# Sample attention reordered: scores of four requests together, values two groups behind, page loads split over two queues

## What is computed

```
# 8 query heads x 64, 2 KV heads, 4 query rows per request: 32 query rows per request
compressed: s = q . kc^T over 255 compressed blocks; p = softmax(s)
            p_grp = sum of p over the 4 heads of a KV head; p_slc = p_grp @ overlap
selected:   idx = top 16 of 65 blocks of 64 tokens (first, last two are forced)
            softmax(q . k^T) . v over the tokens of those blocks, out of 4096 cached and the new ones
window:     softmax(q . k^T) . v over the last 512 cached tokens and the new ones
o = g0 * o_compressed + g1 * o_selected + g2 * o_window
```

## Time and profile before

| | us |
|---|---|
| median of three runs | 3051.97 (3051.2 to 3059.78) |
| the profiled execution | 3054.68 |
| its span, first to last instruction | 3052.6 |
| prompt attention ends (POOL's last instruction) | 1871.5 |
| constants stage, first DMA issue | 1872.6 |
| sample attention, first DMA issue | 1878.0 |
| output projection, first DMA issue | 2109.2 |

### The profile page before, as it was taken

The page is one execution under the profiler, slowest core; times in us unless marked ns, Lnnn a source line. Parts: engine busy times, 40 slices in busy tenths (PEclk is TensorE's granted clock), DMA queues, the critical chain, the costliest instruction groups (busy, mean ns, idle before and its releaser), DMA issues. The chain is left out here.

```text
span 3052.6 us, 46122 instructions
## 1 busy us (share of the span) xinstructions
PE 2769.7 (91%) x17724; PEld 2539.2 (83%) x17724; DVE 1461.4 (48%) x2801; ACT 912.7 (30%) x1600; POOL 343.8 (11%) x362
## 2 busy tenths in 40 slices
PE   4999989999999999899688885876999999999997
PEld 4898978999999999799566663333989999999996
DVE  4444437444444544641377674122264444444445
ACT  4656544111111110323366563333041111111102
POOL 3444430000000000000022223110000000000000
PEclk9999999999999999999789897888999999999999
DMA  4222215111111210213110114544131111111101
GB/s 169 75 102 101 76 65 154 42 41 46 50 41 41 59 37 0 90 58 95 35 47 28 43 42 157 177 145 140 35 97 42 41 41 52 45 41 41 55 0 57
DMA packets 169425, 206.40 MB, mean 68 GB/s; under 512 B 11310, under 2 KB 152495, under 8 KB 166410
## 3 DMA queue, kind: packets, MB, share of 16 engines
q1 hardware_dynamic: 161074, 150.68, 16.2%
q0 software_dynamic: 8224, 54.06, 4.9%
HBM read 190.87 MB, written 18.01 MB: 68 GB/s over the span
## 5 line engine op out<-in xcount | busy, mean ns | idle before, releaser
L406 ACT ACTIVATE f_act_gate<-f_act_gate 128x352 f32<-128x352 f32 x132 | 65.8, 498 | 1186.2 <-DVE f_act_gate L463 1186.2
L500 DVE SCALAR_TENSOR_TENSOR trunk<-f_down,trunk 128x352 f32<-128x352 f32 x528 | 276.0, 524 | 207.6 <-PE f_down L104 207.6
L102 PE MATMUL f_up<-f_h_hi,f_gu_hi 128*128 128x352 f32 x1056 | 344.5, 326 | 0.0
L102 PE MATMUL f_gate<-f_h_hi,f_gu_hi 128*128 128x352 f32 x1056 | 344.3, 326 | 0.0
L104 PE MATMUL f_up<-f_h_hi,f_gu_lo 128*128 128x352 f32 x1056 | 342.7, 325 | 0.0
L104 PE MATMUL f_gate<-f_h_hi,f_gu_lo 128*128 128x352 f32 x1056 | 342.5, 324 | 0.0
L102 PE MATMUL f_down<-f_a_hi,f_wd_hi 128*128 128x352 f32 x1056 | 340.6, 323 | 0.0
L103 PE MATMUL f_gate<-f_h_lo,f_gu_hi 128*128 128x352 f32 x1056 | 340.5, 322 | 0.0
L103 PE MATMUL f_up<-f_h_lo,f_gu_hi 128*128 128x352 f32 x1056 | 340.1, 322 | 0.0
L103 PE MATMUL f_down<-f_a_lo,f_wd_hi 128*128 128x352 f32 x1056 | 338.4, 320 | 0.0
L104 PE MATMUL f_down<-f_a_hi,f_wd_lo 128*128 128x352 f32 x1056 | 338.0, 320 | 0.0
(11 more groups left out here) (359 smaller groups left out, 5457.8 us busy)
## 6 DMA issues: line engine op xcount, KB each, us to landing
as_pages<-in_cache_kv_slc_dram SPq DMA_DIRECT2D x192, 128.0 KB, 2.3
f_gu_raw<-in_w_ffn_gate_dram SPq DMA_DIRECT2D x44, 512.0 KB, 4.2
f_gu_raw<-in_w_ffn_up_dram SPq DMA_DIRECT2D x44, 512.0 KB, 5.5
f_wd_raw<-in_w_ffn_down_dram SPq DMA_DIRECT2D x22, 1024.0 KB, 5.0
at_spread<-saved_rows SPq DMA_DIRECT2D x16, 768.0 KB
as_pages<-in_cache_kv_slc_dram POOLq DMA_DIRECT2D x64, 128.0 KB, 3.4
x_saved<-trunk SPq DMA_DIRECT2D x2, 2112.0 KB, 13.4
trunk<-x_saved SPq DMA_DIRECT2D x1, 4224.0 KB
```

What stands on the lines that cost most here:

```text
L102: pe.matmul(out, w_hi, x_hi, start=first, stop=False)
L406: act.activation(act_gate[:, b, :], act_gate[:, b, :], ACT.Silu).then_inc(silu_done, 1)
L500: dve.scalar_tensor_tensor(xT[:, m, chunk(c)], down_bank[n % 4][:, 0:CH], 0.5, xT[:, m, chunk(c)], ALU.mult, ALU.add).then_inc(down_free, 1)
```

## The change

`stage_attend_sample` is written anew.

- **Order.** The loops over halves and rounds are gone. 18 steps (`STEPS`) run in one straight line: the window of half 0, page groups 0 to 4 of half 0, the window of half 1, page groups 5 to 7 of half 0, then the 8 page groups of half 1. The compressed scores, head sum, choice of blocks and norms of half 1 are put between page groups of half 0, and half 0 is finished (`finish`, `flip`, `place`) during page groups of half 1.
- **Scores.** There are four `kT`, one per request. The step's transposes go in two pairs, and the four score matmuls are issued one behind the other at the end of the step (`key_scores`). ScalarE copies the transposed keys of requests 0 and 1, VectorE those of 2 and 3 (`take_keys`).
- **Values.** The products of step n-2 (`values_of`) stand between the two pairs of transposes of step n. The transposes of the probabilities of step n-1 stand ahead of the scores of step n.
- **Side branch.** The eight small value units become two units of up to 512 columns.
- **Page loads.** SP loads requests 0 and 1, POOL requests 2 and 3: 32 batches each. Page-table addresses are constants, the page numbers are read ahead of the wait for the slot, and the slot is free when the products have been made. The states of half 1 are loaded behind the third page group.
- **Ahead.** `kc`, the gates, `head_sum` and `new_mask` are loaded by SP at the start of prompt attention, and the eight new rows are copied there too. `stage_constants` before sample attention is gone. `win_mask` is loaded at the start of sample attention.
- **Waits.** The idle instructions that TensorE issued to signal the end of a group are gone. Each matmul of a group signals for itself.

The core of the diff:

```diff
             @block.sync
             def _(sp):
+                for target, source in loads_ahead:
+                    sp.dma_start(target, source).then_inc(ahead, 16)
+                for target, source in rows_out:
+                    sp.dma_start(target, source).then_inc(copied, 16)
                 for n in range(TILES):
...
+    SHARE = RQ // 2
+
+    STEPS = ([("w", 0, None)] + [("p", 0, g) for g in range(5)] + [("w", 1, None)]
+             + [("p", 0, g) for g in range(5, KG)] + [("p", 1, g) for g in range(KG)])
...
+    CMP_STEP = [0, 4]
+    SUM_STEP = [0, 5]
+    FLIP_STEP = [LAST_STEP[0] + 4, None]
...
-        kT = [mem.sb(scope, f"as_kT{i}", [P, BANK]) for i in range(2)]
+        kT = [mem.sb(scope, f"as_kT{b}", [P, BANK]) for b in range(RQ)]
...
+        def load_pages(engine, kind, first_request, landed, p):
+            h, g = divmod(p, KG)
+            for b in range(first_request, first_request + SHARE):
+                first = (RQ * h + b) * NP + GP * g
+                _, numbers = nc.values_load_multi_w_load_instructions(
+                    pages[0:1, first:first + GP], [kind], min_val=0, max_val=cache_slc.shape[0] - 1)
+                if p >= RING and b == first_request:
+                    engine.wait_ge(pv_done, values_counted(p - RING))
+                for j, page in enumerate(numbers):
+                    engine.dma_start(page_ring[p % RING][:, b, j, :],
...
-                sp.dma_start(kc[:], kc_dram).then_inc(kc_landed, 16)
+                sp.dma_start(win_mask[:], win_mask_dram).then_inc(mask_landed, 16)
                 sp.dma_start(vc[:], vc_dram).then_inc(vc_landed, 16)
...
-                load_pages(sp, mybir.EngineType.SP, range(RQ - 1), pages_landed)
+                for p in range(PAGES):
+                    load_pages(sp, mybir.EngineType.SP, 0, pages_landed, p)
...
-                load_pages(pool, mybir.EngineType.Pool, [RQ - 1], last_pages_landed)
+                load_state(pool, 0)
+                for p in range(PAGES):
+                    load_pages(pool, mybir.EngineType.Pool, SHARE, more_landed, p)
+                    if p == RING - 2:
+                        load_state(pool, 1)
...
+                exp_cmp(0)
+                for n in range(N):
+                    if n == WIN_STEP[0] + 1:
+                        exp_of(n - 1)
+                    for b in range(SHARE):
+                        take_keys(n, b)
+                    if n > WIN_STEP[0] + 1:
+                        exp_of(n - 1)
+                    if n:
+                        probs_of(n - 1)
+                    if n == CMP_STEP[1]:
+                        exp_cmp(1)
+                exp_of(N - 1)
+                probs_of(N - 1)
...
+                def take_keys(n, b):
+                    dve.wait_ge(kt_turned, RQ * n + b + 1)
+                    dve.wait_ge(s_done, RQ * n)
+                    dve.tensor_copy(kT[b][:], kt_bank[b % 2][:]).then_inc(kt_by_dve, 1)
...
+                for n in range(N):
+                    if n:
+                        max_of(n - 1)
+                    if n == WIN_STEP[0] + 1:
+                        choose_blocks(0)
+                        win_norm(0)
+                    for b in range(SHARE, RQ):
+                        take_keys(n, b)
+                        if b == SHARE and n >= 2:
+                            take_out(n - 2)
...
+                def key_scores(n):
+                    h = STEPS[n][1]
+                    pe.wait_ge(kt_by_act, SHARE * (n + 1))
+                    pe.wait_ge(kt_by_dve, SHARE * (n + 1))
+                    if n >= 2:
+                        pe.wait_ge(s_taken, n - 1)
                     for b in range(RQ):
...
+                        pe.matmul(s_bank[n % 2][rows_of(b), :], queries(RQ * h + b), kT[b][:],
+                                  start=True, stop=True).then_inc(s_done, 1)
...
+                for n in range(N):
+                    if n == CMP_STEP[1]:
+                        cmp_scores(1)
+                    if n == FLIP_STEP[0]:
+                        flip(0)
+                    for b in range(SHARE):
+                        turn_keys(n, b)
+                    if n >= 2:
+                        values_of(n - 2)
+                    for b in range(SHARE, RQ):
+                        turn_keys(n, b)
+                    if n == SUM_STEP[1]:
+                        sum_heads(1)
+                    if n:
+                        probs_of(n - 1)
+                    key_scores(n)
+                values_of(N - 2)
+                probs_of(N - 1)
+                values_of(N - 1)
+                flip(1)
...
+                loads_ahead = [(kc[:], kc_saved), (K["head_sum"][:], c_head_sum), (K["new_mask"][:], c_new_mask)]
+                loads_ahead += [(gate[rows * (b % 4):rows * (b % 4 + 1), b // 4, :],
...
-            stage_constants(nc, mem, [(K["head_sum"][:], c_head_sum), (K["new_mask"][:], c_new_mask),
-                                      (K["win_mask"][:], c_win_mask)] + new_rows)
```

More of the change, by code:

```diff
@@ L2100, in stage_attend_sample @@
[L2100 to L2116, removed]
+        kt_turned, kt_by_act, kt_by_dve = mem.sem("as_kt_turned"), mem.sem("as_kt_by_act"), mem.sem("as_kt_by_dve")
@@ L2118, in stage_attend_sample, with load_state @@
+        def load_state(engine, h):
+            for b in range(RQ):
+                engine.dma_start(state[h][:, b], state_win[RQ * h + b].rearrange("(w p) n -> p w n", p=P)
+                                 ).then_inc(state_landed[h], 16)
         with nc.Block() as block:
@@ L2371, in value_product @@
-                def value_product(hb, n, i, rows, values, bank, first, last):
-                    pe.wait_ge(pt_taken, UNITS * hb + n + RING_TOKENS + 1)
-                    for b in range(RQ):
-                        mm = pe.matmul(bank[ROWS * b:ROWS * (b + 1), 0:P], pT[i][0:rows, ROWS * b:ROWS * (b + 1)],
-                                       values(b), start=first, stop=last)
-                    mm.then_inc(pv_done, 1)
-                def turn_group(hb, g, k):
-                    n = SIDE + 1 + g
-                    pe.wait_ge(exped, SOFT * hb + g + 4)
-                    pe.wait_ge(pt_taken, UNITS * hb + n + 1)
-                    for j in range(GP):
-                        tr = pe.transpose(pt_bank[(SIDE + 1 + k) % 2][:, j * P:(j + 1) * P],
-                                          p_page[k % 2][:, j * P:(j + 1) * P], K["ident"][:])
-                    tr.then_inc(pt_turned, 1)
@@ new lines, in products @@
+                def products(u, bank, terms, first, last, counted=True):
+                    for i, (rows, at, values) in enumerate(terms):
+                        for b in range(RQ):
+                            mm = pe.matmul(bank[rows_of(b), 0:P], pT[u % 2][0:rows, at + ROWS * b:at + ROWS * (b + 1)],
+                                           values(b), start=first and i == 0, stop=last and i == len(terms) - 1)
+                            if counted and i == len(terms) - 1:
+                                mm.then_inc(pv_done, 1)
@@ L2672, in trunk_step @@
         mem.end_stage()
-        with ExitStack() as mixer:
+        ahead, rows_copied = mem.lasting_sem("loaded_ahead"), mem.lasting_sem("rows_copied")
+        with ExitStack() as mixer, ExitStack() as late:
             z_sample = mem.sb(mixer, "z_sample", [P, OFF_POOL])
```

522 lines of the change are left out of this document (275 added, 247 removed).

## The result

The changed kernel takes 0.9708 of the time of the kernel before (95% interval 0.9694 to 0.9723): a median of 2966.3 us against 3054.3, 4 runs each. Run a second time beside other kernels it gave 0.9705 (0.9688 to 0.9722). The profiled execution took 2973.97 us with a span of 2972.1. It was the slowest of its four: prompt attention took 374.7 us in it, and 368.4 in the second profile of the same kernel, against 369.4 before.

What follows compares the result with a forecast made beforehand. Before, a chain of one request after another bound sample attention; after, POOL's page-load issue would. 3054.68 - 5.46 (constants stage) - (231.2 - 144.7) (sample attention) = 2962.7, taken as 2960 us against the runs' median; range 2942 to 2992.

Steps and rivals of the forecast that it cites:

- The constants stage: Ahead of sample attention: removing it saves 5.46 us, its DMA issue moved into SP's idle time in prompt attention at 0 cost.
- The scores side by side: Score matmuls of a step: four requests' pairs run together in 0.9 us plus run-out, with 3.6 as the other bound.
- The step of 5.5 us: Sample attention's new order: one step of computation at full clock, from scores to next scores, takes 5.5 us.
- The computation's floor of 127 us: Sample attention without load limits: 13 + 6 + 93.5 + 5 + 9.6 = 127 us, against 231.2 before.
- POOL sets the pace: Sample attention's page loads: POOL's 32 batches at 3.7 us give 7.4 us per page group, stage 144.7 us; chance 0.62.
- The sign named for POOL's pace: In the profile after: TensorE's third transposes of a step wait for POOL's pages, steps 7.4 us apart.
- The 3 us added for steps that run late: Sample attention: 3 us added to the stage for steps late behind the window steps or at the lower clock, giving 144.7.
- The ring holds: Page slots: 14.8 us from a slot's release to its next use, for 7.4 of issue and 3.4 of landing.
- Rival 1: Sample attention: computation sets the pace through a lower clock or scores in turn, step 8.2 us, time 2991; chance 0.18.
- Rival 2: Page loads: POOL's issue gets dearer under VectorE's copies, 0.67 us per batch, 21 us in all, time 2982; chance 0.07.
- Rival 3: Page loads: POOL's issue is cheaper in straight-line code and not the bound, computation's 127 us stands, time 2942; chance 0.08.
- Rival 4: Slower through the ring: pages landing in above 17.6 us make steps above 12.5 us; 3082 at 20 us landing; chance 0.03.

Runs made afterwards that it cites:

- e8: The changed kernel with a constants stage ahead of sample attention again (head_sum, new_mask, eight new rows): 0.9739 of the kernel before.
- e4: The changed kernel with each of a step's four score matmuls waiting until the one before has ended: 0.9854 of the kernel before.
- e1: The changed kernel with only the first four page groups loaded, all computation kept, output not the reference's: 0.9666 of the kernel before.
- e12: The changed kernel with five slots instead of four in the ring of pages, nothing else: 0.9694 of the kernel before.
- e10: The changed kernel with values behind all four transposes, accumulation behind both key copies, and no bounds checks of page numbers: 0.9712 of the kernel before.
- e11: The changed kernel with values behind all four transposes, accumulation behind both key copies, no bounds checks and a ring of five: 0.9667 of the kernel before.
- e9: The changed kernel with values behind all four transposes and VectorE's accumulation behind both key copies, bounds checks kept: 0.9714 of the kernel before.

## Why the prediction was right, point by point

- **The constants stage**: right. From POOL's last prompt instruction (ending 1878.15) to the first DMA at 1879.19 it is 1.04 us, the barrier alone, where the stage stood. e8 gives 5.0 to it. The cover, SP's idleness in prompt attention, held: SP's first DMA of that stage's own comes 25.1 us after POOL's first instruction there, before (1528.33 - 1503.19) and after (1529.67 - 1504.54).
- **The scores side by side**: right, 1.06 us for 0.9 and run-out. The estimate came from the value products' 0.034 us per instruction, and e4 confirms it.
- **The step of 5.5 us**: right, 5.55 to 5.6 in e1. VectorE's copy took 0.687 against 0.67.
- **The computation's floor of 127 us**: wrong, it is 138.4. The mis-sized term is "5 for the choice of blocks and the norms on VectorE". In e1 the 17 steps take 109.1 us, which is 13.9 more than 17 x 5.6: steps 1 and 2 together 6.1 us, steps 4 to 8 some 8. By its timeline less than a third of that is a wait for VectorE: 2.0 us in step 1, where ScalarE's exponential of the window waits for VectorE's maximum and stands ahead of ScalarE's key copies, 0.6 in step 5 and 0.9 in step 7, where TensorE waits for a norm. About 7 us are TensorE's own instructions, which the sum had at nothing: the compressed scores in step 4 (1.9), the head sum in step 5 (1.1), the window's transposes in step 7 (1.9) and the side branch's value products in steps 2 and 8 (1.15 or so each). Some 3 us in steps 1, 2 and 8 are the low clock: 0.50 was granted from 1895.8 to 1905.2, and the score matmuls at either end of it took 1.94 us. Rows of e1's timeline: the scores of step 3 and the first transposes of step 4, with the compressed scores between them; then step 7, from VectorE's norm over TensorE's window transposes to the scores:

```profile
1918.72 1.07 PE L2461 MATMUL as_s_bank<-as_kT,as_q_diag 128*32 128x512 f32 x8 [1.00 <-issue]
...
1921.60 1.09 PE L2451 MATMUL as_kt_bank<-ident,as_pages 128*128 128x128 f32 x8
...
1944.84 0.50 DVE L2269 TENSOR_SCALAR as_p_win<-as_p_win,as_small 128x544 f32<-128x544 f32 x1
1945.44 0.66 PE L2469 MATMUL as_pt_bank<-ident,as_p_cmp_gated 128*128 128x128 f32 x2 [2.37 <-issue]
...
1946.32 1.06 PE L2469 MATMUL as_pt_bank<-ident,as_p_win 128*128 128x128 f32 x4
...
1947.31 1.60 PE L2461 MATMUL as_s_bank<-as_kT,as_q_diag 128*32 128x512 f32 x8
```

- **POOL sets the pace**: half right at most. The batch was 3.65 us, between the bounds 3.6 and 3.81. But one step in which the prediction goes wrong is "a stream that never waits": computation was behind it up to step 9, so the slots of the ring came late, and POOL lost 7.8 us. Only from step 11 on did TensorE wait for pages. The other is that SP was left out of it, at 115 us against POOL's 118.4. The sign named for POOL's pace, TensorE waiting ahead of the third transposes, shows in steps 14 to 16 alone. From step 11 on it waited ahead of the first (6.9 of 9.0 us), for SP's pages. My working of why, from these numbers: both streams start again at the same freed slot, SP's 6.9 us per group is too slow for the step as well and its pages are due 2.0 us earlier, and POOL's 7.3 falls behind it by only 0.4 us per group. No run changed SP's stream alone at two requests each, so that stays an argument. The stage was 147.3 for a forecast of 144.7, since two errors met: loads that set the pace in seven steps and not in all, and a floor 11 us higher. That the time came within 6 us is luck in that part. The 3 us added for steps that run late stood for 7.8.
- **The ring holds**: the sentence compared 14.8 us with 10.8, at steps of 7.4. At the steps of 5.6 that computation made between 9 and 12 it is 11.2 against 7.3 + 3.4 = 10.7, which leaves next to nothing. e12 shows the loss and e10 what happens when the values come later still.
- **Rival 1**, computation as the pace through a low clock or scores in turn: the clock was 0.92 and 1.00 where it had been 0.96 and 0.92. Over whole windows neither condition came, though single steps ran at 0.50 (above). Computation was the pace in ten of the 17 steps without needing either.
- **Rival 2**, POOL's issue dearer beside VectorE's copies: refuted. Four issues take 2.29 us next to 36 copies, as they did without them. The Trainium skill's "SBUF — State Buffer", "SBUF: two separate sides", lets a VectorE operation in a two-port mode keep GpSimd from writing descriptors, and its "VectorE: DVE Perf Modes", "Why PSUM operands drop a tier", keeps an fp32 copy out of PSUM from that mode. The 2.29 agrees.
- **Rival 3**: e1 shows that even without the later loads it is only 2953 or so, not 2942.
- **Rival 4**, slower: POOL's pages landed in 3.4 us as before, SP's in 3.3 where it had been 2.3, and in e11 POOL's in 4.5, far from 17.6.

The Trainium skill's "TensorEngine Tiling (Array Packing)", in "Performance Considerations", says that after a fourfold speed-up the copies out of PSUM may become the limit, and that both ScalarE and VectorE should share them. The trace agrees with the first part: the score matmuls fell from 77.5 to 20.7 us busy, and in a step of 5.6 TensorE stands idle for 1.0 us ahead of the scores, which start when VectorE's second key copy has ended.

What each part is worth, where it was taken alone out of the changed kernel: scores side by side 45 us, the loads' division 50, the constants stage 5 by its length (10 by the times, which don't settle it). They overlap and don't add up to the 89. The order of the rest (values two groups behind, second side branch between pages, no emptying every four groups) wasn't taken out by itself. e4 gives a bound: with the scores in turn the new order still had 192.8 us against 236.6.

## What to carry to other kernels

When a chain gets shorter, price what feeds it at the new pace: the time of each issuing stream per item, not of the slowest alone, and the time from a buffer's release to its next use against the steps between them, at the shortest step and not at the mean. Where two streams feed a step, the faster one is the limit if its goods are due earlier by more than it is ahead. An edit that makes the step shorter but frees buffers later (e9, e10) can bring nothing until one more buffer is there. And count every small instruction that is put into the stream of an engine on the chain: its cover is gone as soon as that engine is what the next step waits for.

## What the runs showed of the hardware that was not expected

- Reading four page numbers costs POOL's stream 1.35 us with bounds checks and 0.40 without. Its four DMAs of 128 KB take 2.29 us to issue, with 36 VectorE copies beside them or none.
- Matmuls on the four quarters of 32 columns overlap fully when they are issued one behind the other, also those that stand in the trace as two instructions: eight in 1.06 us, against 4.33 in turn.
- The DMA engines carried 372 GB/s over 32 us at a share of 1.05 in e11, and the median landing of POOL's 128 KB rose from 3.4 to 4.5 us. A row of e11's table of windows, with the columns of the first table above:

```profile
1958.00:1990.00 32.00, 29.77 (x391) 20.07 (x395) 23.23 (x58) 17.60 (x41) 24.00 (x45) 1.00 1.05 372
```

And of its DMA issues (out<-in, queue, operation, count, KB each, median us from issue to landing):

```profile
as_pages<-in_cache_kv_slc_dram POOLq DMA_DIRECT2D x128, 128.0 KB, 4.5
```
